# Other walks over the 512 token columns in the matmuls of the five MLPs

## The reference, cut to what matters

```
def squared_relu_mlp(h, w_in, w_out):             # mlp0, mlp1: 1024 -> 4096 -> 1024
    return jnp.square(jax.nn.relu(h @ w_in)) @ w_out

def swiglu(h, w_gate, w_up, w_down):              # ffn1, ffn2: 1024 -> 2816 -> 1024, with norms
    return (jax.nn.silu(h @ w_gate) * (h @ w_up)) @ w_down

def swiglu_ffn(h, w_ffn_in, w_ffn_out):           # ffn3: the same widths
    gate, up = jnp.split(h @ w_ffn_in, 2, axis=-1)
    return (jax.nn.silu(gate) * up) @ w_ffn_out
```

## Time and profile before

| what | us or share |
|---|---|
| median of two runs | 3553.39 |
| span of the profiled execution | 3546.6 |
| TensorE busy | 3392.8 (96%) |
| GpSimd busy | 1896.5 (53%) |
| VectorE busy | 1649.7 (47%) |
| ScalarE busy | 747.6 (21%) |
| mean granted TensorE clock | 0.982 |
| bytes moved by DMA, mean rate | 340.83 MB, 96 GB/s |

### The profile page before, as it was taken

One profiled execution on the slowest core, in us unless ns is written; L12 is line 12 of the kernel. 1 busy time (PEld: TensorE's weight loads), 2 busy tenths in 40 slices (PEclk: granted clock), 3 DMA queues, 4 the chain that ended last, 5 costly groups with the idle time before them and its releaser, 6 DMA issues.

```text
span 3546.6 us, 47349 instructions
## 1 busy us (share of the span) xinstructions
PE 3392.8 (96%) x19819; PEld 2682.2 (76%) x19819; DVE 1649.7 (47%) x2892; ACT 747.6 (21%) x1636; POOL 1896.5 (53%) x1495
## 2 busy tenths in 40 slices
PE   8989999999999999999999888999999998989998
PEld 6767888886678887888788677778887775768886
DVE  4344334548743445333452655464346657541123
ACT  2241111245521012000102522110002224220001
POOL 6516756840066667676665001776665620746663
PEclk9999999999999999999999989999999999999999
DMA  4203333230023333332233001422224533413221
GB/s 163 78 7 114 112 131 131 85 102 25 1 84 107 131 131 119 96 118 95 95 95 110 11 2 56 136 93 93 95 95 158 198 111 131 143 63 104 95 92 40
DMA packets 253686, 340.83 MB, mean 96 GB/s; under 512 B 9760, under 2 KB 186144, under 8 KB 250912
## 3 DMA queue, kind: packets, MB, share of 16 engines
q1 hardware_dynamic: 230960, 301.51, 25.9%
q10 hardware_dynamic: 22512, 36.28, 3.0%
HBM read 308.15 MB, written 25.43 MB: 94 GB/s over the span
## 4 chain that ended last, share of the span: by engine, by line
PE 70%; DVE 7%; ACT 2%; POOL 1%; issue 1%; DMA 0%; ACTq 0%; DVEq 0%; POOLq 0%
PE bank L113 68%; PE bank L116 2%; DVE scr L136 1%; DVE al L146 1%; POOL wlo L136 1%; DVE rb L136 1%; ACT ah L131 0%; DVE st L151 0%; DVE scr L146 0%; DVE x L136 0%; DVE p L143 0%; ACT L131 0%; POOL whi L143 0%; DVE BK L136 0%; ACT p L131 0%
## 5 line engine op out<-in xcount | busy, mean ns | idle before, releaser
L143 POOL TENSOR_SCALAR whi<-raw 128x1024 fp32r<-128x1024 f32 x481 | 550.4, 1164 | 1579.7 <-PE bank L113 898.9
L136 POOL TENSOR_TENSOR wlo<-raw,whi 128x512 fp32r<-128x512 f32 x962 | 1302.9, 1386 | 20.1
L113 PE MATMUL bank<-ah,whi 128*128 128x512 f32 x2408 | 960.4, 399 | 24.7 <-POOL wlo L136 11.6
L113 PE MATMUL bank<-ah,wlo 128*128 128x512 f32 x2408 | 952.9, 396 | 0.0
L113 PE MATMUL bank<-al,whi 128*128 128x512 f32 x2408 | 941.5, 396 | 0.0
L113 PEld LDWEIGHTS bank<-ah,whi 128*128 128x128 f32 x2408 | 452.7, 188 | 147.0 <-POOL wlo L136 11.1
L113 PEld LDWEIGHTS bank<-al,whi 128*128 128x128 f32 x2408 | 452.4, 188 | 111.0 <-issue 1.4
L113 PEld LDWEIGHTS bank<-ah,wlo 128*128 128x128 f32 x2408 | 452.4, 188 | 110.3 <-issue 0.2
L113 PE MATMUL bank<-hh,whi 128*128 128x512 f32 x1040 | 412.4, 397 | 0.0
L113 PE MATMUL bank<-hl,whi 128*128 128x512 f32 x1040 | 410.8, 395 | 0.0
L113 PE MATMUL bank<-hh,wlo 128*128 128x512 f32 x1040 | 410.7, 395 | 0.0
(11 more groups left out here) (431 smaller groups left out, 4057.8 us busy)
## 6 DMA issues: line engine op xcount, KB each, us to landing
raw<-in_w_in SPq DMA_DIRECT2D x34, 1024.0 KB, 5.2
raw<-in_w_mlp_in SPq DMA_DIRECT2D x32, 1024.0 KB, 5.6
raw<-in_w_mlp_out SPq DMA_DIRECT2D x32, 1024.0 KB, 6.3
raw<-in_w_ada SPq DMA_DIRECT2D x24, 1024.0 KB, 5.4
raw<-in_ffn_w_gate SPq DMA_DIRECT2D x22, 1024.0 KB, 5.3
raw<-in_ffn_w_up SPq DMA_DIRECT2D x22, 1024.0 KB, 5.3
raw<-in_ffn_w_down SPq DMA_DIRECT2D x22, 1024.0 KB, 5.0
raw<-in_w_ffn_in SPq DMA_DIRECT2D x22, 1024.0 KB, 5.0
```

Of the source, the lines that this page charges most:

```text
L113: return self.eng.matmul(out, lhsT, rhs, start=start, stop=stop, skip_group_check=True)
L136: return IDLE if self.eng is None else self.eng.tensor_tensor(out, a, b, op)
L143: return self.eng.tensor_scalar(out, a, s1, s2, op0, op1)
```

## The change

`lin` now passes both the moving operand and the bank through a new function, `in_turn`. For the five MLPs it views the 512 columns as `parts` stretches of equal length, and walks them in turns: `piece` columns of the first stretch, `piece` of the second, and so on, then the next `piece` columns of the first. Both views have the same order, so each column of the result goes to the address it had before. Nothing else is changed: the same instructions are issued in the same order with the same waits, DMAs and tiles, and all readers of the banks are as they were.

| MLP | parts, piece | walk | run | runs |
|---|---|---|---|---|
| mlp0 | 2, 4 | 4 columns of each half in turn | 16 bytes | 128 |
| mlp1 | 2, 64 | 64 columns of each half in turn | 256 bytes | 8 |
| ffn1 | 2, 2 | 2 columns of each half in turn | 8 bytes | 256 |
| ffn2 | 4, 8 | 8 columns of each quarter in turn | 32 bytes | 64 |
| ffn3 | 128, 2 | columns 0, 1, then 4, 5, 8, 9 to 508, 509; then 2, 3, 6, 7 to 510, 511 | 8 bytes | 256 |

```
+    COLUMNS = {"mlp0": (2, 4), "mlp1": (2, 64), "ffn1": (2, 2), "ffn2": (4, 8), "ffn3": (128, 2)}
+
+    def in_turn(self, name, tile):
+
+        if not isinstance(name, tuple) or name[0] not in self.COLUMNS:
+            return tile
+        parts, piece = self.COLUMNS[name[0]]
+        return tile.rearrange("p (h a j) -> p a h j", h=parts, j=piece)
+
     def lin(self, e, name, W, r0, kt, cols, act, ready=None, staggered=True, after=None,
...
                 for k in range(kt):
-                    ah, al = act(k)
+                    ah, al = (self.in_turn(name, x) for x in act(k))
...
                     for i, bank in zip(turn, banks):
-                        s = slice(128 * i, 128 * i + 128)
-                        e.mm(bank[:, :], hi[:, k, s], ah, k == 0, False)
-                        e.mm(bank[:, :], hi[:, k, s], al, False, False)
-                        t = e.mm(bank[:, :], lo[:, k, s], ah, False, k == kt - 1)
+                        s, out = slice(128 * i, 128 * i + 128), self.in_turn(name, bank[:, :])
+                        e.mm(out, hi[:, k, s], ah, k == 0, False)
+                        e.mm(out, hi[:, k, s], al, False, False)
+                        t = e.mm(out, lo[:, k, s], ah, False, k == kt - 1)
```

## The result

The changed kernel takes 4062.32 us, the median of two runs (4053.13 and 4071.51), against 3553.39 us: a ratio of 1.1442, with a 95% interval of 1.1421 to 1.1464. The span of its profiled execution is 4069.7 us, 523.1 us more than that of before. The forecast was 4261 us, in a range of 3545 to 4300 us, so the direction held and the size was 200 us too high.

A forecast was written before the change was run, and what follows sets the result against it. TensorE's gapless matmul streams were taken as the bound. Span 3546.6 + 369.6 (ffn1) + 347.2 (ffn3) - 9 = 4254 us, plus 6.8 us for runs over profiled span: 4261 us; range 3545 to 4300 us.

The forecast's parts named there:

- The bound: Whole kernel: TensorE, busy 3392.8 of 3546.6 us; each MLP a gapless matmul stream, so the distance between starts counts.
- mlp1: 0 us: mlp1, runs of 64: all whole fetches, 128 per matmul as before, so 0 us added.
- ffn3: 347 us: ffn3, runs of 2: 256 fetches instead of 128, 233.3 ns more for each of 1488 matmuls, 347.2 us.
- ffn1: 370 us: ffn1, runs of 2: 256 fetches instead of 128, 233.3 ns more for each of 1584 matmuls, 369.6 us.
- only one of the two pair orders pays: Rival, chance 0.09: ffn1 free through kept groups, 3896 us; or ffn1 alone pays, 3916 us.
- mlp0 and ffn2: 0 us: mlp0 (runs of 4) and ffn2 (runs of 8): whole fetches, 128 per matmul as before, 0 us added.
- What a fetch is: Moving operand: TensorE fetches four neighbouring columns (16 bytes) per 1.82 ns, however many of the four it uses.
- The bound from the weight loads: Lower price of a fetch, from weight loads with a step: 1.70 ns, 435 ns a matmul, +620 us.
- Writing to the bank: 0 us: Output with gaps in all five MLPs: taken as free; from above another 233.3 ns for each matmul.
- Every order pays: Rival, chance 0.08: bank write or step between runs costs as much as the read; all five MLPs halve, +1803 us, 5350 us.
- Pairs are enough (0.18): Rival, chance 0.18: the stream is fed two columns at a time, all five orders keep pairs, time stays 3553 us.
- What comes back: 9 us: ffn1 and ffn3: waits for GpSimd and VectorE that vanish, and matmuls already slow at the lower clock, return about 9 us.

The follow-up runs named there:

- 4x2: Changed kernel with other orders, operand and bank: ffn1 walked as 4 parts in pieces of 2 columns; 447 ns between matmul starts.
- 16x2: Changed kernel with other orders, operand and bank: ffn3 walked as 16 parts in pieces of 2 columns; 433 ns between matmul starts.
- 2x1: Changed kernel with other orders, moving operand alone, bank contiguous: ffn1 walked as 2 parts in pieces of 1 column; 216 ns between matmul starts.
- 32x4: 32 parts in pieces of 4, operand and bank: 220 ns in ffn1, again in ffn3; in all five MLPs 3472.88 us, 0.9787 of the kernel before.
- 128x1: Changed kernel with other orders, moving operand alone, bank contiguous: mlp1 walked as 128 parts in pieces of 1 column; 462 ns between matmul starts.
- 128x2: The changed kernel's own ffn3 order, 128 parts in pieces of 2 columns; 453 ns between matmul starts, also with the moving operand alone permuted.
- 64x2: Changed kernel with other orders, moving operand alone, bank contiguous: ffn3 walked as 64 parts in pieces of 2 columns; 462 ns between matmul starts.

## Why the prediction was right or wrong

**The bound.** Right. The MLPs are one gapless stream on TensorE, and the time of the change is the sum of the distances: 530 us by the trace, 523 us in the span, and 37 against 38 us with the pairs undone. The other engines' work stayed, and the clock in ffn1 and ffn3 stayed at 0.99 to 1.00.

**mlp1: 0 us.** Right, 233 ns.

**ffn3: 347 us.** Right but for 20 us. 220.0 ns more for each matmul instead of 233.3, 327 us. The step of one new fetch for each pair held. The price was 453 / 256 = 1.77 ns a fetch and not 1.82; by the reading above it is 4 cycles, 1.67 ns, and 27 ns a matmul on top.

**ffn1: 370 us.** The step that failed, in size. It added 166 us, 204 less than forecast; with ffn3 20 less and mlp0 and ffn2 together 37 more, that is the miss of the forecast. The prediction counted 256 fetches as in ffn3 and took no line as kept. With halves in turn each line is used again after one other. If the second visit costs 2 cycles and not 4, that is 128 x (4 + 2) = 768 cycles, and with the 48 that a contiguous matmul has on top 816, the measured 340 ns. The 48 are borrowed: the same order with 480 columns took 17 on top of 720. That a reuse is what makes it cheap is borne out by 4x2 and 16x2, where the reuse comes later and the distance is 447 and 433 ns; how it does so no view shows. The rival "only one of the two pair orders pays" named just this mechanism. It had it make ffn1 free; it made ffn1 about half price, as if a new line weren't fetched ahead while a kept one is read.

**mlp0 and ffn2: 0 us.** Too low, by 29 and 8 us (18.7 and 5 ns). The prediction took any order of whole lines for as good as contiguous. The runs show 220 to 279 ns for such orders, and the size goes neither by the number of jumps nor by their length alone.

**What a fetch is.** The one number, 1.82 ns a fetch, fitted three rows and by the runs was still two effects: some 4 cycles for a line (1.67 ns), which a contiguous stream just hides, and 20 ns lost in a contiguous matmul for another reason, which stays open. That this loss isn't the fetch is shown by 216 ns with 2x1 and 220 ns with 32x4, which read the same 128 lines. The bound from the weight loads, 1.70 ns, was the better one. The count "one fetch for each piece of four, however many are used" was right for pieces of two whose line isn't soon used again, and wrong for single columns: 128x1 touches 512 lines and takes 462 ns.

**Writing to the bank: 0 us.** Right: 233 ns in all five MLPs with the bank alone permuted. "Every order pays" is gone. Of the two sentences of the Trainium skill ("Advanced Engine Details and Errata", "Memory Cachelines") the one on pairs agrees, in that pairs are enough (single columns on the bank weren't tried), and the one on any access that isn't contiguous doesn't.

**Pairs are enough (0.18).** Gone for the moving operand. The two hits in a line that the same section of the Trainium skill asks for aren't enough in the walk, as 128x2 takes 453 ns. By the reading of two readers they fit if each reader needs its two, which makes four columns of the walk, as in a contiguous one.

**What comes back: 9 us.** About 7 us, by the sum of the distances against the span. In ffn1 the 2.6 us of waiting for GpSimd are gone, with the stretch at the lower clock behind them, and at its end the 2.8 us for VectorE's `al`; the 5.3 us in front of ffn3's second slab stayed, as said.

## What to carry to other kernels

The order in which a matmul walks its moving operand is cheap only in whole 16-byte lines, and even there it can cost up to a fifth (279 against 233 ns): in fp32, a piece of four columns that begins at a multiple of four. Pieces of two, or pieces of four that begin off the line, cost up to about twice the time (453 and 462 against 233 ns for 512 columns), while the bank may be written in pairs at no cost. Before putting a price on such an access, find out whether a line is used again soon, and measure it in the stage itself, more than once: the small part (220 to 279 ns among orders of whole lines) followed no rule found here and changed between two executions.

## What the runs showed of the hardware that was not expected

A contiguous fp32r stream isn't the fastest. 512 columns take 233 ns contiguous, 216 ns when two lines are walked in turn column by column (2x1, and 0, 4, 1, 5, ...), and mostly 220 to 225 ns with 32x4, which gave a kernel 2.1% faster (95% interval 2.0 to 2.3%). In the 216 ns case only the moving operand was permuted; a kernel that uses it would have to store its activations in that order, or write the bank in single columns, and neither was tried. Two columns of a walk seem to be read side by side: 128x1 with 512 line visits costs 462 ns, like 64x2 with 256. At the lower clock a stream that is bound by its reading costs the same, 453 ns at 0.50 and at 1.00.
